# The tensor engine's drains behind blocks of split products go; the weight split waits on the matmuls' own increments

## The reference

```python
proj = rmsnorm(h) @ w_in          # 1024 -> gates (3 x 1024) | RWKV | S5 | Mamba (z, xBC, dt)
o_r = rwkv7(...)                  # recurrence per head, samples with their own states
o_s = s5(...)                     # gelu, then y * sigmoid(y @ w_glu), then @ w_out_s5
o_m = mamba2(...)                 # norm, then @ w_out_mamba
merged = sig(g_r) * o_r + sig(g_s) * o_s + sig(g_m) * o_m
h += rmsnorm(merged @ w_out);  h += rmsnorm(cross_attend(h));  h += rmsnorm(relu(h @ w1)**2 @ w2)
```

## Time and profile before

| | |
|---|---|
| three runs | 4606.02, 4606.3, 4618.85 us; median 4606.3 |
| span of the profiled execution | 4613.1 us |
| TensorE (PE) busy | 4125.8 us, 89% of the span, 35797 matmuls |
| VectorE busy | 2521.4 us, 55% |
| ScalarE busy | 1557.5 us, 34% |
| GpSimd busy | 222.5 us, 5% |
| split products of `pz`, `pa`, `pb` (L210) | 984 + 384 + 816 triples |
| split products of the branch sums (L1717) | 768 triples |

### The profile page before, as it was taken

How to read it: one execution, slowest core, us unless ns; L and a number is a source line. 1 busy time by engine, 2 the same in 40 slices (tenths; PEclk the granted TensorE clock), 3 DMA queues, 4 the chain that set the end, 5 groups by cost and what they waited for, 6 DMA issues and landing times. The chain is left out here.

```text
span 4613.1 us, 84517 instructions
## 1 busy us (share of the span) xinstructions
PE 4125.8 (89%) x35797; PEld 3766.7 (82%) x35797; DVE 2521.4 (55%) x4994; ACT 1557.5 (34%) x2536; POOL 222.5 (5%) x161
## 2 busy tenths in 40 slices
PE   8789999989899999778768888886998899999998
PEld 4779989889888888778757777776976889999997
DVE  3344646332278884377846777764553255444446
ACT  3112222231176663221114555543541253111113
POOL 0000000000011110121200000000001100000000
PEclk9899999989899999889979999997999899999999
DMA  4322222233355553545530000004222221111112
GB/s 171 86 87 85 83 85 88 68 96 113 102 150 152 159 143 120 147 126 179 166 124 23 31 24 28 31 10 155 98 98 85 79 84 64 46 47 46 42 33 76
DMA packets 374262, 418.69 MB, mean 91 GB/s; under 512 B 49162, under 2 KB 315964, under 8 KB 373020
## 3 DMA queue, kind: packets, MB, share of 16 engines
q1 hardware_dynamic: 361599, 368.01, 26.1%
q0 software_dynamic: 7680, 27.97, 2.0%
q10 hardware_dynamic: 4608, 17.30, 0.9%
HBM read 289.10 MB, written 121.77 MB: 89 GB/s over the span
## 5 line engine op out<-in xcount | busy, mean ns | idle before, releaser
L1717 PE MATMUL bank<-sum_x_hi,sum_w_hi 128*128 128x352 f32 x768 | 262.3, 342 | 100.3 <-DVE sum_x_lo L1700 39.8
L210 PE MATMUL bank<-xn_hi,pz_whi 128*128 128x352 f32 (+1 forms) x984 | 328.4, 334 | 20.6 <-DVE pz_wlo L195 14.5
L210 PE MATMUL bank<-xn_hi,pz_wlo 128*128 128x352 f32 (+1 forms) x984 | 319.9, 325 | 0.0
L210 PE MATMUL bank<-xn_lo,pz_whi 128*128 128x352 f32 (+1 forms) x984 | 318.3, 323 | 0.0
L224 ACT ACTIVATE ring<-bank 128x352 f32<-128x352 f32 (+1 forms) x273 | 125.6, 461 | 541.4 <-PE bank L210 541.1
L3065 PE MATMUL bank<-bx_hi,bp_whi 128*128 128x384 f32 (+1 forms) x768 | 275.3, 358 | 32.7 <-DVE bx_lo L3123 19.7
L210 PE MATMUL bank<-xn_hi,pb_whi 128*128 128x352 f32 x816 | 275.1, 337 | 20.1 <-DVE pb_wlo L195 14.2
L210 PE MATMUL bank<-xn_lo,pb_whi 128*128 128x352 f32 x816 | 266.0, 326 | 0.0
L210 PE MATMUL bank<-xn_hi,pb_wlo 128*128 128x352 f32 x816 | 265.3, 325 | 0.0
L3686 PE MATMUL bank<-bx_hi,bp_whi 128*128 128x384 f32 (+1 forms) x768 | 251.7, 328 | 4.7 <-issue 4.7
L1717 PE MATMUL bank<-sum_x_hi,sum_w_lo 128*128 128x352 f32 x768 | 255.8, 333 | 0.0
(11 more groups left out here) (710 smaller groups left out, 12440.7 us busy)
## 6 DMA issues: line engine op xcount, KB each, us to landing
ring<-in_w_in_dram SPq DMA_DIRECT2D x90, 512.0 KB, 4.8
proj_scratch<-ring SPq DMA_DIRECT2D x66, 528.0 KB, 3.0
m_seg<-acum_scratch SPq DMA_DIRECT2D x32, 512.0 KB, 6.8
ring<-in_mlp_w_dram SPq DMA_DIRECT2D x16, 1024.0 KB, 5.5
ring<-in_mlp_w_dram SPq DMA_DIRECT2D x32, 512.0 KB, 3.4
gates_scratch<-ring SPq DMA_DIRECT2D x24, 528.0 KB, 4.6
merged_scratch<-sum_gate ACTq DMA_DIRECT2D x24, 528.0 KB, 5.1
m_raw<-proj_scratch SPq DMA_DIRECT2D x24, 512.0 KB, 5.7
```

Source lines behind the costliest of these rows:

```text
L210: last = self.nc.tensor.matmul(ps[0:n, 0:m], w[:, q, 0:n], self.pair[x][:, q, t0:t0 + m], start=q == 0 and j == 0, stop=q == KD - 1 and j ...
L1717: last = self.nc.tensor.matmul(self.banks[e % n][:, 0:m], w[:, b % 2, q, :], self.pair[x][:, q, t0:t0 + m], start=q == 0 and i == 0, stop= ...
```

## The change

The drains at L213 and L1720 and the semaphore `used` are removed. `high` of block b now waits until `product` has reached 3 (b - 1), which is the increment of the last matmul of block b-2. In `S5Input` the drain at L347 is removed: the last matmul of each of the first seven triples raises `freed` itself; the eighth, which already raises `product`, raises nothing more, and the split of tile 7 waits for `product` at Q5 + 1. The lines in between are the same, and so are all DMAs and the weave's due times.

```diff
@@ Columns
-        self.w_hi, self.w_lo, self.used, self.product, self.off = S("w_hi"), S("w_lo"), S("used"), S("product"), S("off")
+        self.w_hi, self.w_lo, self.product, self.off = S("w_hi"), S("w_lo"), S("product"), S("off")
             if b >= 2:
-                act.wait_ge(self.used, b - 1)
+                act.wait_ge(self.product, 3 * (b - 1))
             n = self.width(b)
                 last.then_inc(self.product, 1)
-            pe.drain().then_inc(self.used, 1)
@@ S5Input
             for q in range(KD):
-                if s:
+                if s and q < KD - 1:
                     act.wait_ge(self.freed, q + 1)
+                elif s:
+                    act.wait_ge(self.product, Q5 + 1)
                 self.nc.scalar.activation(self.hi[:, q, :], self.raw[:, s, q, :], ACT.Copy).then_inc(self.w_hi, 1)
-                    if i == Q5 and s == 0:
-                        pe.drain().then_inc(self.freed, 1)
+                    if i == Q5 and s == 0 and q < KD - 1:
+                        last.then_inc(self.freed, 1)
                 last.then_inc(self.product, 1)
```

More of the change, by code:

```diff
@@ L1597, in __init__ @@
         self.loaded, self.stored, self.gate_in, self.prev_in, self.x_in = two("loaded"), three("stored"), three("gate_in"), three("prev_in"), two("x_in")
-        self.w_hi, self.w_lo, self.used, self.product, self.done, self.x_hi, self.x_lo, self.sig = (
-            S("w_hi"), S("w_lo"), S("used"), S("product"), S("done"), S("x_hi"), S("x_lo"), S("sig"))
+        self.w_hi, self.w_lo, self.product, self.done, self.x_hi, self.x_lo, self.sig = (
+            S("w_hi"), S("w_lo"), S("product"), S("done"), S("x_hi"), S("x_lo"), S("sig"))
         self.off = [S(f"off{i}") for i in range(len(banks))]
```

## The result

The changed kernel took 4585.83 us (median of 6 runs, 4576.62 to 4592.54) against 4606.43 (6 runs, 4601.19 to 4622.49) for the kernel before; the ratio is 0.9947, with an interval of 0.9932 to 0.9963. It is faster by 20.6 us, where I forecast 43.4, and 3.8 us above the upper end of the range. Two more groups of six runs, each beside runs of the kernel before, gave 4576.01 (ratio 0.9936, 0.9923 to 0.9949) and 4573.33 (0.9933, 0.9916 to 0.995). The median of all 18 runs of it is 4577.2. That of 49 runs of the kernel before (r_before, r_before2 and the 25 beside the last experiments) is 4605.7, 28.5 us more; all 78 that the experiments list give 4605.4. So part of the miss is the kernel's own spread, and most of it is not.

What follows compares the result with a forecast made beforehand. TensorE was taken to set the pace in most of the five changed stretches; savings of 2.0 + 16.8 + 5.5 + 10.3 + 8.8 = 43.4 us off the median 4606.3 gave 4562.9 us, range 4550 to 4582.

Steps and rivals of the forecast that it cites:

- What a drain costs: At TensorE's block ends: a drain costs 0.50 us, or 0.33 to 0.43 where another helper's product follows.
- the middle case: At block ends, only the idle time shown, 0.26 of the 0.50 us, goes: 22 us saved, 4585; chance 0.06.
- rival (b): At block ends, the cost lies in a block's opening and stays with its two waits: 4606 us; chance 0.04.
- S5 input: Eight drains behind triples of one chunk, 0.25 us each: 2.0 us saved, all kept.
- Scan stage: Columns beside the S5 scan: 21 x 0.50 + 19 x 0.33 = 16.8 us saved, all kept.
- First Mamba part: Columns beside the first Mamba part: 3 x 0.50 + 12 x 0.33 = 5.5 us saved, all kept.
- Branch sums: Last changed stretch: 14.8 us priced, 12 of 31 block ends (6.0 us) lost to waits, 8.8 kept.
- The stop before the ninth block: In the branch sums: TensorE's 18 us stop there would become longer by about 1 us.
- the 4.0 us lost to other engines in the second Mamba part: There 9 of 33 block ends only reach the same wait earlier: 4.0 of 14.3 us lost, 10.3 kept.
- rival (a): Second Mamba part and branch sums: VectorE and the recurrence set the pace and take much more: 4576 us; chance 0.12.
- Everything from the end of the branch sums on is unchanged: All stages behind the branch sums: the profile after would show no change there.
- Rival (c): Branch sums, first Mamba part: longer TensorE stops lower the clock; 5 points cancel the gain, 8 give about 4625; chance 0.02.

Runs made afterwards that it cites:

- r_before: The kernel before, unchanged, run again: 4607.6 us, ratio 1.0006.
- r_before2: The kernel before, unchanged, run once more: 4605.26 us, ratio 0.9999.
- e_chunk: The kernel before with a drain also behind the other two chunks of each block, 246 more drains: 4689.31 us, ratio 1.0178.
- e_pz: The kernel before with the change in the scan stage's run of Columns alone, all other drains kept: 4594.0 us, ratio 0.9973.
- r_after: The changed kernel, run again: 4576.01 us, ratio 0.9936 to the kernel before.
- a_free: The changed kernel with 131 TensorE drains added at the front, in S5Params, where TensorE stands still: 4568.75 us, ratio 0.9915 to the kernel before.
- e_sums: The kernel before with the change in the branch sums and the S5 input alone; Columns keeps its drains: 4605.41 us, ratio 0.9998.
- a_pad: The changed kernel with 131 TensorE drains and a barrier added between the branch sums and RWKV: 4583.36 us, ratio 0.9947 to the kernel before.

## Why the prediction was wrong, by its own steps

**What a drain costs** was right as a sum: 0.50 us between two products of a block, 0.42 of them in the first step and 0.08 in the second, all gone with the drain, so that the middle case (0.26 of 0.50) and rival (b) fall with the timeline. The reason given for it, that "a drain is all that differs" and the two waits are free, was not quite right. They are free where no drain stands ahead; behind a drain the second costs 0.09 us, and with the increment 0.50 is reached from 0.37 (e_chunk). As both effects go with the drain, the sum doesn't suffer. The Trainium skill's "TensorE: Matmul & The Clock Gate", section "Single matmul latency", with its 166 ns, would have given 21 us by my estimate, and the first median lies right beside it. That is chance: the steps in the timeline have lost 0.50 us, and the 246 further drains cost 84.6 us, where 166 ns each would be 41 (an estimate from the same section).

**The terms.** S5 input: 2.0 forecast, 2.8 found (2.4 over the profiles). Scan stage: 16.8 against 15.4, and 16.3 in e_pz. First Mamba part: 5.5 against 2.3, but 5.7 between the profiles of r_before and r_after, and 10.5 between those of before and a_free. Its block ends lose 5.4 us in the first pair, so the term is right, and the rest is what the clock adds or takes: the half clock in this stage is 68 to 86 us in the profiles of the kernel before and 64 to 83 in those of the changed one. Branch sums: 8.8 against 9.3. These hold. The stop before the ninth block, for which I forecast 1 us more, went from 17.95 to 17.07 in this pair and from 16.99 to 17.85 in that of r_before and r_after, so it shows nothing.

**The step that was mis-sized** is the 4.0 us lost to other engines in the second Mamba part. In all 8.2 us were missing in the first pair (14.3 priced, 6.1 found), and about 7 over all profiles; 5.9 of them stand in the list as new or longer waits. (The prediction calls VectorE "nearly as full as TensorE" there; its own have 74% against 94%.) I had counted block ends that stand before a wait which the profile of before shows. But in other places, where no wait showed yet, earlier products ran into new ones: 2 waits at L2734 became 6. That is rival (a), at about half its size and in one of its two stages. It is worth 3 to 4 us, 2 of them shown as waits.

**The step that failed** is "Everything from the end of the branch sums on is unchanged", and with it the sum, which had no term for the granted clock. Rival (c) had the resource and a wrong mechanism: it let the clock fall only if TensorE's stops grew in the changed stretches, and asked for 5 points. It fell by 0.4 points over the 18 runs (0.54 in the first six), spread over most stages, the untouched ones among them, and by the account this took some 12 to 14 us (17 to 19). In the first pair of profiles 7.9 us came back behind the branch sums. Its own test, that the clock's share falls in the last two stretches, came out at 0.98 to 0.97 in the one and 0.90 as before in the other: it looked in the wrong place, as RWKV, the back end and attention took more.

**The range.** 4582 was worked out from absorption alone. With 20 us for the clock and 4 more for absorption it would have reached some 4587. My 0.3% for what can be told from no change was right for the difference of two medians; that the medians of six runs of one kernel can themselves stand 10 or 12 us apart (4585.8, 4576.0, 4573.3), I had not allowed for.

**What stays open.** Why the mean clock goes down when stalls go. In one stage a part of it is shown: a moved instruction fetch lets TensorE restart earlier, and a pad that brings the fetch back takes the two pieces of half clock away, in both kernels that have one. That the restart makes them is not shown, as e_sums has it without them. a_free restores TensorE's place in its stream from RWKV on, and its mean clock is the nearest to before; that the same cause is at work in other stages is a guess. It also moves the fetches of the stages ahead, a_pad has the clock at 0.948 with the back end restored, and e_sums, which moves the stream by only 40 instructions, has it as low as 0.9481. And the Mamba part's half clock differs between executions of one kernel. None of the runs holds the clock fixed, so the 14 us are an account, not an isolated effect, and some of them may be other costs that come with a lower clock.

## What to carry to other kernels

Replace a drain that only frees a buffer by the increment of the last matmul: here that was worth 0.17 to 0.50 us at each place where TensorE sets the pace, and showed no cost. But take the clock into the sum of a TensorE kernel with thin stages: in the first pair of profiles it stood at the lower level for 464 us before and 496 after, and stages whose code is the same had become longer. And count absorption not only where a wait shows: where the next engine is at three quarters, 5.9 us of a gain of 14.3 went into waits that were new or longer.

## What the hardware showed that I had not expected

An instruction fetch competes with the data. One packet of 16 KB in a burst of loads goes with a stop that is 1.1 us longer, in nine profiles of nine, and whether it falls into the burst depends on how many instructions stand before it: 131 do-nothing drains in idle time moved it, and made a stage 3 ms later 2.2 us shorter. The kernel was some 8 us faster with them, of which only these 2.2 have a place in the trace.

To go on sooner was not faster. In eight profiles the stage that restarted 1.1 us earlier ended 2.2 us later against its start; in the ninth it ended 0.7 us earlier.

A drain is not one price. Between the same two products it cost 0.37 us with one met wait behind it, 0.46 with two, and 0.50 with two and an increment of its own, while the waits and the increment cost nothing without it.

The time of one and the same kernel goes with its mean clock, by 3.2 to 3.6 us for each 0.001 (correlation 0.86 and 0.93), which is most of the spread: 4570.07 us at 0.949 and 4592.54 at 0.944 for the changed kernel.
